# The residual of the last token block moved ahead of the first half's chunks at three joints of a two-layer decoder trunk

## The reference

```
h  = x * (1 + scale) + shift            # input of the next sub-layer
y  = sublayer(h)                        # last step: a product with w_out or w2
x  = layer_norm(ALPHA * x + (1 + gate) * y, g, b)
```

## Time and profile before

| | us |
|---|---|
| median of 3 runs | 1514.02 (1513.11 to 1518.57) |
| the profiled execution, its own time | 1514.3 |
| its span | 1512.5 |
| TensorE busy in the span | 1375.6 |
| VectorE busy | 615.0 |
| ScalarE busy | 442.9 |
| GpSimd busy | 509.7 |
| mean granted TensorE clock | 0.957 of full speed |

### The profile page before, as it was taken

How to read it: one execution, slowest core, us unless ns; L and a number is a source line. 1 busy time by engine, 2 the same in 40 slices (tenths; PEclk the granted TensorE clock), 3 DMA queues, 4 the chain that set the end, 5 groups by cost and what they waited for, 6 DMA issues and landing times.

```text
span 1512.5 us, 17029 instructions
## 1 busy us (share of the span) xinstructions
PE 1375.6 (91%) x6510; PEld 1124.3 (74%) x6510; DVE 615.0 (41%) x817; ACT 442.9 (29%) x595; POOL 509.7 (34%) x209
## 2 busy tenths in 40 slices
PE   1789979798999999999999999986889999999995
PEld 1568767577888888788788778746779888887884
DVE  5854813667744333400683133136576111010006
ACT  0332323324322322211322243332333322322112
POOL 0432522032444443544235233200125444444440
PEclk9989989899999999999999999997999999999998
DMA  9269442051365464753315512101013323234311
GB/s 362 96 169 71 141 138 84 0 194 71 112 213 177 165 220 153 251 111 98 106 61 210 151 56 83 43 1 56 29 56 98 98 85 109 87 84 149 98 56 55
DMA packets 87024, 173.79 MB, mean 115 GB/s; under 512 B 15367, under 2 KB 53399, under 8 KB 86844
## 3 DMA queue, kind: packets, MB, share of 16 engines
q1 hardware_dynamic: 83832, 169.62, 36.8%
q10 hardware_dynamic: 3140, 3.43, 0.8%
HBM read 170.87 MB, written 4.52 MB: 116 GB/s over the span
## 4 chain that ended last, share of the span: by engine, by line
PE 63%; issue 23%; DVE 6%; POOL 6%; ACT 2%; POOLq 0%; DVEq 0%; ACTq 0%
PE ps L978 12%; PE ps L979 12%; PE ps L980 12%; PE ps L1010 6%; PE ps L1011 6%; PE ps L1012 6%; POOL w_lo L647 6%; PE ps L1377 1%; PE ps L1101 1%; PE ps L1102 1%; PE ps L1103 1%; PE ps L1349 1%; PE ps L1360 1%; PE ps L1363 1%; DVE rec L2010 1%
## 5 line engine op out<-in xcount | busy, mean ns | idle before, releaser
L647 POOL TENSOR_TENSOR w_lo<-raw,w_hi 128x1024 fp32r<-128x1024 f32 x205 | 509.5, 2489 | 967.4 <-ACT w_hi L667 967.1
L978 PE MATMUL ps<-h_lo,w_hi 128*128 128x512 f32 (+2 forms) x1064 | 404.5, 380 | 21.5 <-POOL w_lo L647 7.0
L979 PE MATMUL ps<-h_hi,w_hi 128*128 128x512 f32 (+2 forms) x1064 | 400.0, 376 | 0.0
L980 PE MATMUL ps<-h_hi,w_lo 128*128 128x512 f32 (+2 forms) x1064 | 399.6, 376 | 0.0
L667 ACT ACTIVATE w_hi<-raw 128x1024 fp32r<-128x1024 f32 x205 | 216.0, 1056 | 522.7 <-DMA raw<-wstream 189.6
L978 PEld LDWEIGHTS ps<-h_lo,w_hi 128*128 128x128 f32 (+1 forms) x1064 | 205.4, 193 | 63.3 <-issue 10.9
L980 PEld LDWEIGHTS ps<-h_hi,w_lo 128*128 128x128 f32 (+1 forms) x1064 | 205.0, 193 | 35.5
L979 PEld LDWEIGHTS ps<-h_hi,w_hi 128*128 128x128 f32 (+1 forms) x1064 | 205.4, 193 | 33.8
L1010 PE MATMUL ps<-w_hi,hid_lo 128*128 128x512 f32 x352 | 140.0, 398 | 1.8 <-issue 0.9
L1011 PE MATMUL ps<-w_hi,hid_hi 128*128 128x512 f32 x352 | 139.6, 396 | 0.0
L1012 PE MATMUL ps<-w_lo,hid_hi 128*128 128x512 f32 x352 | 139.5, 396 | 0.0
(11 more groups left out here) (219 smaller groups left out, 1430.5 us busy)
## 6 DMA issues: line engine op xcount, KB each, us to landing
raw<-wstream SPq DMA_DIRECT2D x205, 512.0 KB, 4.1
ada_raw<-astream SPq DMA_DIRECT2D x80, 512.0 KB, 4.4
ada_first<-astream SPq DMA_DIRECT2D x4, 2048.0 KB, 15.1
ln_rows<-row_scratch SPq DMA_DIRECT2D x3, 1024.0 KB, 6.6
skew_scratch<-f_scratch ACTq DMA_DIRECT2D x1, 2304.0 KB
xa<-xT SPq DMA_DIRECT2D x2, 1024.0 KB, 18.4
out<-xa SPq DMA_DIRECT2D x4, 512.0 KB, 3.5
gate_mixer<-row_scratch SPq DMA_DIRECT2D x2, 512.0 KB, 5.5
```

The source lines that it names most:

```text
L647: nc.gpsimd.tensor_tensor(w_lo[:, slot, :], raw[:, slot % RAW, :], w_hi[:, slot, :].bitcast(F32), ALU.subtract).then_inc(sem("w_lo_ready"), 1)
L978: pe.matmul(o, w_h, x_l, start=start, stop=False)
L979: pe.matmul(o, w_h, x_h, start=False, stop=False)
L980: return pe.matmul(o, w_l, x_h, start=False, stop=stop)
```

## The change

The residual of token block 3 is done right behind those of blocks 0 to 2 on VectorE, ahead of the eight chunks of half 0, and ScalarE normalises block 3 right behind block 2, ahead of the weight slots and the h_hi chunks. The code of TensorE, GpSimd and the DMA queues is the same, and the last sub-layer's end (i = 3) keeps its order.

```diff
@@ scalar engine, norm(i, name, following)
-            for tb in range(3):
+            for tb in range(TB):
                 normalize(tb)
             if following is None:
-                normalize(3)
                 return
             n0 = SLOTS[following][0]
             hi_until(n0 + 1)
...
                     hi_until(n0 + 2)
                 if n == 5:
                     hi_until(n0 + 3)
-            normalize(3)
             hi_until(n0 + 4)
             for n in range(KC):
                 hi_of_half(i, 1, n)
@@ vector engine, norm(i, name)
                 if i == 3 and tb:
                     dve.wait_ge(sem("in_rows"), 16)
                     affine(tb - 1, rows_gb, sem("out_ready"))
+            residual(3)
             if i < 3:
                 half_chunks(i, 0)
-            residual(3)
             if i == 3:
                 affine(2, rows_gb, sem("out_ready"))
                 affine(3, rows_gb, sem("out_ready"))
```

## The result

| | median us | lowest to highest | runs |
|---|---|---|---|
| before | 1513.88 | 1512.86 to 1518.57 | 6 |
| changed | 1530.4 | 1523.89 to 1532.8 | 6 |

The changed kernel is slower, by a ratio of 1.0095 (95% interval 1.0073 to 1.0118; the two medians alone give 1.0109). Its profiled execution took 1530.58 us, with a span of 1528.8 and a mean granted clock of 0.952 (before: 1512.5 us and 0.957). The same code timed once more on another chip gave 1531.04 us against 1513.63, a ratio of 1.0113 (1.0081 to 1.0144).

A forecast was written before the change was run, and what follows sets the result against it. TensorE was taken to bound the kernel, so its idle time at joints adds almost one to one. 24.39 - 5.70 - 2.1 - 0.8 = 15.8 us on 1514.3 gave 1530.1; forecast 1526 to 1536 (0.80), range 1525 to 1537.

The forecast's parts named there:

- The delay of q0: At the three joints, q0 starts later by as much as block 3's L827 follows block 2's old time: 24.39 us.
- What lets q0 go: In front of each q0, TensorE's idle time of 10.2 us would be ended by h_lo or w_lo.
- The wait that goes: In front of turn(i, 1), TensorE's waits vanish since block 3 is normalised before q0: 5.70 us gained.
- VectorE's later work: In half 1 and the affine blocks behind, VectorE runs about 1.2 us earlier: 2.1 us gained, bounds 0 and 2.5.
- The granted clock: In q0, no net clock cost, bounds +2.0 and -2.5 per joint; joint 2's second slow stretch goes, 0.8 us gained.
- rival A: TensorE stays at 1.2 GHz through all of q0, VectorE gives nothing back: 1538.2 us; with times beyond 1536, chance 0.09.
- q0 has about as many slow matmuls as it has now: In q0 at each joint, the clock rises some 4 us behind chunk 1, so its cost is taken as 0.
- The lower bound: In q0, all 45 matmuls behind chunk 0 at 0.12 us would make it 7.4 us, 2.5 less at each joint.
- The sum: Over the whole kernel, the terms add 15.8 us to 1514.3, giving 1530.1; 1530 us predicted for the median.
- B: Behind the joints, part of the delay is made good later: 1524.4 us; with times from 1521.6 to 1526, chance 0.06.
- C: At the joints, removed waits outweigh q0's delay, so faster: 1505.7 us with no delay at all; chance 0.02.
- D: In half 0, chunks already wait until about the same time for their transposes, so no change: 1514 us; chance 0.03.

The follow-up runs named there:

- experiment 1: The changed kernel's new order at joint 1 alone, the other joints as in the kernel before: 1517.8 us, ratio 1.001 to the kernel before.
- experiment 3: Changed kernel, with w_hi of slots n0 and n0+1 made ahead of block 3's normalisation: 1516.17 us, ratio 1.0018 to the kernel before.
- experiment 4: As experiment 3, with block 3's L827 moved behind the third h_hi: 1514.62 us, ratio 1.0006 to the kernel before.
- experiment 2: Changed kernel, with w_hi of all four slots n0 to n0+3 made ahead of block 3's normalisation: 1516.16 us, ratio 1.0017 to the kernel before.
- experiment 9: Kernel before, with the edits of experiment 6 and experiment 7 together: 1508.05 us, ratio 0.9954 to the kernel before.
- experiment 5: Changed kernel, with nine unused matmuls on constants added in TensorE's gap at each joint: 1528.84 us, ratio 1.008 to the kernel before.
- experiment 6: Kernel before, with w_hi of slot n0+3 made ahead of block 3's normalisation: 1509.54 us, ratio 0.9969 to the kernel before.
- experiment 7: Kernel before, with block 2's L827 moved behind the third h_hi: 1508.78 us, ratio 0.9956 to the kernel before.
- experiment 8: Kernel before, with turn(i, 1) two matmul groups later: 1512.18 us, ratio 0.9982 to the kernel before.
- experiment 10: Kernel before, with the edits of experiment 6, experiment 7 and experiment 8 together: 1505.16 us, ratio 0.9934 to the kernel before.

## Why the prediction was right

1530.0 was predicted, 1530.4 measured, and the sign, the mechanism and the place were as forecast. By its own steps:

*The delay of q0* was put at 24.39 us and is 24.47. Moving q0's start by the difference of the two L827 was right because the chain behind it kept its order and overlaps: L827 to q0 is 360.01 - 354.57 = 5.44 us before and 369.54 - 364.13 = 5.41 now. Experiment 1 shows the delay at one joint alone, and experiment 3 that the gap falls to 7.36 when the slots move out of the chain.

*What lets q0 go* was put at h_lo or w_lo. It is the fourth tmp, about half a microsecond behind the first h_lo, before and after the change: the earlier trace rows name it too. The forecast did not suffer, since the whole chain was moved as it stood, but the expectation of experiment 4 did.

*The wait that goes* was put at 5.70 us, and all three waits are gone.

*VectorE's later work* is a term that was mis-sized: 2.1 us expected, and the two gaps that it named give about 0. Its first half came true: the first h_lo of half 1 takes 0.41 us, and ScalarE's L866 waits 6.59 us instead of 7.71. But at joint 0 TensorE's gap grew from 0.89 to 1.40 us, and at joint 1 it fell only from 1.63 to 1.10. The expected gaps were under 0.5. TensorE and ScalarE in the changed kernel:

```profile
416.83 0.47 PE L976 MATMUL ps<-h_lo,w_hi 128*128 128x512 f32 x1 [1.40 <-ACT w_hi L667]
...
797.72 0.76 PE L976 MATMUL ps<-h_lo,w_hi 128*128 128x512 f32 x1 [1.10 <-issue]
```

```profile
403.95 1.23 ACT L866 ACTIVATE hid_hi<-tmp 128x512 fp32r<-128x512 f32 x2 [6.59 <-DVE tmp L1858]
413.18 1.06 ACT L667 ACTIVATE w_hi<-raw 128x1024 fp32r<-128x1024 f32 x1 [8.00 <-DMA raw<-wstream]
```

and the issue of that slot's DMA on SyncE, changed kernel first, kernel before second:

```profile
407.13 1.54 SPq L587 DMA_DIRECT2D raw<-wstream  x1
```

```profile
400.11 0.33 SPq L587 DMA_DIRECT2D raw<-wstream  x1
```

ScalarE is early, but the weights come from a DMA whose issue took 1.21 us longer, so the 1.12 us were gone. This issue took 1.27 us in the repeat of the changed kernel (gap 0.90), and 1.30, 1.57 and 1.60 in experiments 2, 4 and 9 (gaps 1.02, 0.56 and 1.06); it took 0.33 in experiments 3, 5 and 6 (gap 0.41, none and none). Among the traces whose first h_lo of half 1 is short, the long issue thus goes with the larger gap; what makes it long was not tried. Nor is a growth of 0.51 us much more than what two executions of the same code differ by: in experiment 1, whose code at joint 0 is that of the kernel before, the gap is 1.33 instead of 0.89, with an issue of 0.33. At joint 1 the gap is 1.10 to 1.12 us in the changed kernel, its repeat and experiments 1 to 6, all with a short h_lo, so the short h_lo buys 0.5 us there and not the 1.2 that I had put on it. What the rest waits for stays open; it is not fixed, for experiment 7 has 0.53 there.

*The granted clock* was put at 0 in q0, and -0.8 at joint 2. The windows of joints 0 and 1 in the changed kernel:

```profile
370.00:377.00 7.00, 5.97 (x27) 5.52 (x27) 5.34 (x11) 3.35 (x6) 4.00 (x2) 0.50 0.80 301
378.00:381.00 3.00, 3.00 (x29) 3.00 (x28) 0.39 (x1) 0.00 (x0) 2.02 (x1) 1.00 0.52 175
765.00:770.00 5.00, 3.97 (x17) 3.53 (x17) 5.00 (x11) 2.77 (x6) 2.00 (x2) 0.50 0.95 358
771.00:774.00 3.00, 3.00 (x28) 3.00 (x27) 0.00 (x0) 0.00 (x0) 3.00 (x2) 1.00 0.22 44
```

q0 began at 1.2 GHz and the clock came back to 2.4 within it, as forecast, so rival A did not happen. But the slow part is not the same as before: at joint 0 it lasts from q0's start to 377, over 7 us, where before the clock was back at 367, 7 us behind q0's start, with the slow windows from 363.5. The step "q0 has about as many slow matmuls as it has now" failed there: 27 matmuls stand in 370 to 377, against 14 in 363.5 to 366.5. q0 takes 10.36, 9.34 and 10.49 us, against 9.70, 9.70 and 9.53, so 1.26 more in all, where 0 was taken and 6.0 and -7.5 were the bounds. (The lower bound was also summed wrongly: its 7.4 us leave out the transpose that the 9.97 hold.)

The second slow stretch at joint 2 is gone, but it was worth twice the 0.8. The prediction had cut out 2.5 us of it. A wider window of TensorE in the kernel before (length, busy, granted clock, DMA share, GB/s):

```profile
1134.50:1138.00 3.50, 3.50 (x19) 0.51 0.11 14
```

Behind the second transpose of turn(2, 1) the changed kernel gains 1.6 us on the kernel before while this stretch passes.

*The sum.* TensorE runs the same instructions in the same order in both traces, so the start of each in the kernel before can be taken from its start in the changed one. This lag, in us, with the times of the kernel before:

| where | lag |
|---|---|
| last matmul ahead of joint 0 (358) | 1.0 |
| q0, then behind turn(0, 1) (374) | 9.5, 8.1 |
| 500, then 630 | 8.6, 7.3 |
| q0, then behind turn(1, 1) (764) | 15.3, 12.8 |
| 800, then ahead of joint 2 (1110) | 11.4, 11.1 |
| q0, then behind the stretch at 1138 (1140) | 19.1, 16.3 |
| the end | 16.3 |

Term by term, measured against forecast: the delay of q0 is 24.5 us (24.4); the waits that go give 6.2 (5.7), counted from the start of the transpose ahead of each wait to the start of the one behind it; q0 itself costs 1.3 (0); behind the joints 1.0 is gained (2.1), a loss of 0.5 behind joint 0 and a gain of 1.45 behind joint 1; the slow stretch gives 1.6 (0.8), and the turns 0.1 (0). These make 16.9 us where 15.8 was forecast. Away from the joints stand 1.0 us of lag ahead of joint 0, 1.3 less at 619 and 0.3 less behind 800, which leaves 16.3.

Behind joint 1 only 0.5 of the 1.45 us is the shorter gap. Most of the rest, and the 1.3 us at 619, are slow stretches. Windows of TensorE, first of the kernel before, then of the changed one, then of experiment 1:

```profile
619.00:623.00 4.00, 3.32 (x9) 0.57 0.39 112
...
784.00:790.00 6.00, 4.37 (x11) 0.51 0.07 14
```

```profile
622.00:632.00 10.00, 9.14 (x49) 1.00 0.37 119
...
797.50:801.00 3.50, 3.28 (x8) 0.51 0.00 0
```

```profile
619.00:623.00 4.00, 3.13 (x15) 1.00 0.25 73
790.00:793.50 3.50, 3.50 (x9) 0.51 0.07 9
```

The stretch at 619 is absent in the changed kernel, and also in experiment 1, whose code up to joint 1 is that of the kernel before: it is a difference between executions. The stretch behind joint 1's affine blocks is half as long, and this repeats: it is short in all seven traces with the new order at joint 1 (the changed kernel, its repeat, experiments 1 to 5), and long in the kernel before and in experiments 6, 8 and 10. Experiments 7 and 9, in the old order, have the short one too, so the new order is not the only way to it; why it shortens was not tried.

The match of 1530.0 with 1530.4 is thus closer than the terms were, by luck: VectorE's later work and the clock in q0 missed by 2.4 us one way, the waits and the slow stretch by 1.3 the other way, and the differences away from the joints took 0.6 more.

*The rivals:* A needs q0 of over 11 us and B a later stage that gives back more than the 2.1 us of the forecast; neither is in the traces. C and D fall with the gaps.

## What to carry to other kernels

Work that waits for the end of a bottleneck engine's last job must not stand, on an in-order engine, in front of work which that engine's next job needs; the price can be read beforehand as the distance from that end to where the chain can start, less the waits that go. If it must stand there, move whatever needs nothing of it (here the split of the weight slots) ahead of it: experiment 3 lost 2.5 us where the changed kernel lost 17.4 beside it. Before taking back a gain from an engine that becomes early, look at what else ends at the same place (a DMA's issue, a read of another bank): an early ScalarE only changed who ended the wait. Look for gains on the same chain, from its other side: half a normalisation moved behind three chunks gave 7.3 us here. And ask of every start what really ends the wait: here it was a bank that an instruction behind the expected one had to read.

## What the hardware showed that I had not expected

GpSimd's w_lo beside VectorE holds even an instruction of one element per partition: L1820 took 1.54 us beside it in experiment 2, and the same instruction 0.16 without it in experiment 3. The Trainium skill (SBUF — State Buffer, Who interferes with whom) states that a VectorE instruction with two SBUF inputs contends with a GpSimd instruction that reads SBUF, and the trace of experiment 2 agrees down to 128x1.

Keeping TensorE busy in the gap brought its clock to 2.4 GHz at the start of q0 and did not shorten q0 (10.42 us against 10.36 at joint 0); the clock fell again inside q0, behind waits of 2.52 and 1.42 us (experiment 5).

The issue of a weight DMA on SyncE took 0.33 us in some traces and 1.27 to 1.60 us at the same place in others (407.13 in the changed kernel).
